# Two attentions with sinks: half of a query projection moved inside the heads, bias rows stored elsewhere, other step tables in two further attentions

## The chip, the cores and the metric

One core of one Trainium2 chip runs the whole program. The metric is the time of one execution on the device, in microseconds (us). TensorE (PE, with its weight loads as PEld), VectorE (DVE), ScalarE (ACT) and GpSimd (POOL) each walk an order of their own; SyncE (SP) issues the weight transfers.

## The reference

Two models one after the other, over 256 tokens of width 1024. The first has four layers: a mixer, a layer norm, a swiglu feed-forward (inner width 2816) and a layer norm. Layers 0 and 3 mix by `mixer_a`, windowed attention with 16 query heads, 4 key/value heads and a learned sink per head; layer 1 is a dilated attention in three groups (`mixer_b`), layer 2 a full causal one (`mixer_c`). Two hybrid layers follow, which the change leaves in their order. Of `mixer_a`:

```python
def mixer_a(x, w_qkv, b_qkv, sinks, w_o, b_o, cos, sin):
    B, S, _ = x.shape
    nq, nkv = A_HEADS * HEAD_DIM, A_KV_HEADS * HEAD_DIM
    qkv = x @ w_qkv + b_qkv
    q = apply_rope(qkv[..., :nq].reshape(B, S, A_HEADS, HEAD_DIM), cos, sin)
    k = apply_rope(qkv[..., nq:nq + nkv].reshape(B, S, A_KV_HEADS, HEAD_DIM), cos, sin)
    v = qkv[..., nq + nkv:].reshape(B, S, A_KV_HEADS, HEAD_DIM)
    o, _ = block_attention(q, k, v, WIN_BLK, A_WINDOW - 1, True, sinks)
    return o.reshape(B, S, nq).astype(x.dtype) @ w_o + b_o
```

The sink is a logit that joins each head's maximum and denominator.

## The kernel before, in words

**Products.** The tokens are two row tiles (t = 0, 1) of 128. A weight chunk is 1024 rows by 512 columns; SP brings it to one of three slots of `raw`. A float32 product is taken as three: the chunk is split into a rounded `whi` (ACT, L1292, half a chunk at a time, or POOL, L1226, in quarters) and the rest `wlo` (DVE, L1715, half a chunk), the rows of x likewise, and each of 8 K-steps is three matmuls of 128x512 (hi·hi, lo·hi, hi·lo). So a projection of one row tile is 24 matmuls, of both 48: L2561 in `product`, or L2577 in `three`, by which a layer's first products and the output projection go.

**One list of stages.** The host code adds stages to a list written by hand; every engine walks the list in order and takes its own part of each stage, tied to the others by semaphores. Nothing is reordered at run time: what stands behind a waiting instruction on its engine waits too.

**Attention with sinks.** Three chunks: one with keys and values, two with queries. After each, DVE adds the bias from PSUM (`biased`, L1821, with the row `abias` in the large buffer `arena`) and rotates the first quarter of every head (`rotated`, L1840 to L1843, in the scratch rows `r`); PE turns the heads (`turn_heads`, L2528, PSUM banks T0 and T1), and ACT copies them into `arena` (L1313). DVE also adds the output bias `abo` to x (L1982). The last query chunk is projected for both row tiles ahead of the heads. Then `spread` does the heads, one unit per head, in 20 steps:

- even step i: PE `scores_of_two(i)` for units i and i+1 (L2793), which takes two of the banks S0, S1, L0, L1 in turn;
- DVE `maxima(i)` (L2093 sets the sink's columns, L2098 adds the mask and takes the maximum), `reciprocal(i-1)` (L2111), `copies(i-3)` (L2106, from a T bank to `pts`);
- ACT exponentials (L1485) and the first scale (L1493), POOL the second scale (L1235);
- PE `turned(i-3)` (L2804), and in odd steps `values_of_two` (L2817) of a pair whose two copies are in.

A bank is free when its reader is done: a T bank when DVE's or ACT's copy is, an S or L bank when both maxima of its unit are. After each four heads ACT rounds the group (L1320) and DVE takes the rest (`group_low`, L1736). `parts` are pieces of the output projection that PE does inside the heads, `rest` those behind them; `lows` and `splits` say in which step DVE splits which chunk.

**Dilated and full.** `paired` does heads in pairs (scores, L2734 turned, L2755 values, DVE's copies L2213); `fill` gives the steps over which a projection is spread inside the heads, as a triple (first step, end of row tile 0, end of row tile 1).

**Between layers.** `renorm` normalises row tile 1 last (DVE L1790, which raises `x_ready`), while PE is already at the next layer's first products of row tile 0; PE then turns x (L2516), and DVE takes xt's low half (L1729) before PE can go on with row tile 1.

## Time and profile before

| | |
|---|---|
| median of 3 runs | 2402.16 us (2400.73 to 2404.18) |
| the profiled execution | 2401.17 us |
| its span | 2399.0 us |
| TensorE's granted clock | 1.00 of full speed |
| PE busy | 2354.6 us, 98% |
| DVE busy | 1636.2 us, 68% |
| ACT busy | 1137.8 us, 47% |
| POOL busy | 225.4 us, 9% |

The span runs from the first to the last instruction that the profiler records. The busy shares are averages over unlike stages; the idle time of PE, by place, is what they leave out.

### The profile page before, as it was taken

Reading aid. Unit: us, or ns where it says so; the run is one execution under the profiler, and the core shown is the slowest. Engines: PE = TensorE matmul, PEld = TensorE weight load, DVE = VectorE, ACT = ScalarE, POOL = GpSimd, SP = SyncE. Lnnn points to the kernel's source line nnn. Section 1 sums busy time; section 2 is a strip of 40 time slices with the busy share of each in tenths; the row PEclk is TensorE's granted clock in tenths of the full one; section 3 lists DMA queues with packets and bytes.
Section 4 is the critical chain, followed back from the end, with each engine's and each line's share of the span. In section 5 each row is a group of like instructions: output and inputs, shape, how many; then the busy total and the mean of one; then the engine's idle time right before and its main releaser. Section 6 shows DMA issues by size and latency. Waiting matters only on the chain.

```text
span 2399.0 us, 31702 instructions
## 1 busy us (share of the span) xinstructions
PE 2354.6 (98%) x12768; PEld 1980.5 (83%) x12768; DVE 1636.2 (68%) x2282; ACT 1137.8 (47%) x1523; POOL 225.4 (9%) x238
## 2 busy tenths in 40 slices
PE   7999999999999999998999999999999999999999
PEld 6788888887888778886888888888888888988887
DVE  7766755557667676677776777777676577687664
ACT  5543345554433544435443455564444365574442
POOL 2400002012000220003100100100100001001000
PEclk9999999999999999999999999999999999999999
DMA  6465343335553455643754344444755344445652
GB/s 250 143 204 207 141 176 141 141 141 176 202 202 141 176 176 193 211 147 122 263 195 174 137 176 159 158 177 148 280 187 182 119 162 158 174 176 186 226 173 91
DMA packets 259072, 418.97 MB, mean 175 GB/s; under 512 B 11984, under 2 KB 149200, under 8 KB 258928
## 3 DMA queue, kind: packets, MB, share of 16 engines
q1 hardware_dynamic: 254064, 400.15, 47.1%
q0 software_dynamic: 4864, 16.80, 2.2%
q8 instruction: 103, 1.69, 0.3%
q14 instruction: 41, 0.34, 0.0%
HBM read 415.86 MB, written 1.05 MB: 174 GB/s over the span
## 4 chain that ended last, share of the span: by engine, by line
PE 89%; DVE 5%; ACT 2%; DMA 1%; issue 1%; POOL 0%; SPq 0%; DVEq 0%; ACTq 0%
PE bank_L L2561 19%; PE bank_L L2577 16%; PE bank_S L2981 8%; PE bank_T L2946 7%; PE bank_L L2946 7%; PE bank_O L2981 7%; PE bank_L L2558 4%; PE bank_T L2951 4%; PE bank_L L2951 4%; PE bank_S L2577 1%; DVE wlo L1715 1%; PE bank_S L2561 1%; PE bank_O L2561 1%; PE bank_T L2528 1%; PE bank_T L2516 1%
## 5 line engine op out<-in xcount | busy, mean ns | idle before, releaser
L1715 DVE TENSOR_TENSOR wlo<-raw,whi 128x2048 fp32r<-128x2048 f32 x316 | 717.5, 2290 | 119.6 <-ACT whi L1292 119.1
L1292 ACT ACTIVATE whi<-raw 128x2048 fp32r<-128x2048 f32 x290 | 542.3, 1894 | 46.8 <-DMA raw<-in_w_in 12.5
L2561 PE MATMUL bank_L<-whi,xt 128*128 128x512 f32 (+2 forms) x1632 | 495.2, 386 | 0.9 <-DVE wlo L1715 0.8
L2577 PE MATMUL bank_L<-whi,xt 128*128 128x512 f32 x1152 | 359.3, 393 | 2.5 <-DVE xt L1729 1.8
L2561 PEld LDWEIGHTS bank_L<-whi,xt 128*128 128x128 f32 x1632 | 296.5, 188 | 57.7 <-issue 2.8
L2561 PE MATMUL bank_L<-wlo,xt 128*128 128x512 f32 (+2 forms) x816 | 311.6, 382 | 0.0
L1587 ACT ACTIVATE tok<-tok 128x256 f32<-128x256 f32 x96 | 40.1, 417 | 449.7 <-DVE tok L2267 449.7
L2577 PEld LDWEIGHTS bank_L<-whi,xt 128*128 128x128 f32 x1152 | 213.3, 188 | 48.0 <-issue 2.7
L2577 PE MATMUL bank_L<-wlo,xt 128*128 128x512 f32 x576 | 225.0, 391 | 0.0
L2946 PE MATMUL bank_T<-xt,whi 128*128 128x512 f32 x768 | 192.4, 393 | 0.0
L2946 PE MATMUL bank_L<-xt,whi 128*128 128x512 f32 x768 | 191.8, 392 | 0.0
L2267 DVE TENSOR_REDUCE tok<-bank_L 128x256 f32<-128x512 f32 x96 | 66.3, 691 | 175.8 <-PE bank_L L2951 175.8
L2561 PEld LDWEIGHTS bank_L<-wlo,xt 128*128 128x128 f32 x816 | 153.5, 188 | 30.1
L2946 PEld LDWEIGHTS bank_L<-xt,whi 128*128 128x128 f32 x768 | 140.8, 189 | 26.9
L2946 PEld LDWEIGHTS bank_T<-xt,whi 128*128 128x128 f32 x768 | 138.3, 189 | 24.6
L2253 DVE TENSOR_TENSOR dlo<-draw,dhi 128x1024 fp32r<-128x1024 f32 x132 | 155.4, 1219 | 3.4 <-ACT dhi L1577 3.4
L1577 ACT ACTIVATE dhi<-draw 128x1024 fp32r<-128x1024 f32 x132 | 131.4, 1045 | 0.0
L2577 PEld LDWEIGHTS bank_L<-wlo,xt 128*128 128x128 f32 x576 | 108.2, 188 | 22.9
L2558 PE MATMUL bank_L<-xt,whi 128*128 128x256 f32 x640 | 118.1, 286 | 0.0
L2267 DVE TENSOR_REDUCE tok<-bank_T 128x256 f32<-128x512 f32 x96 | 66.0, 688 | 74.1 <-PE bank_T L2951 74.1
L1343 ACT ACTIVATE tok<-bank_L 128x512 f32<-128x512 f32 x68 | 40.5, 597 | 152.3 <-PE bank_L L2561 105.9
L2951 PEld LDWEIGHTS bank_L<-xt,wlo 128*128 128x128 f32 x768 | 104.8, 190 | 7.5
(380 smaller groups left out, 3792.2 us busy)
## 6 DMA issues: line engine op xcount, KB each, us to landing
raw<-in_w_gate_up SPq DMA_DIRECT2D x176, 512.0 KB, 5.5
raw<-in_w_in SPq DMA_DIRECT2D x72, 1024.0 KB, 6.8
draw<-in_w_down SPq DMA_DIRECT2D x44, 1024.0 KB, 6.1
raw<-in_ffn_w_up SPq DMA_DIRECT2D x88, 512.0 KB, 5.6
raw<-in_b_w_qkv SPq DMA_DIRECT2D x36, 1024.0 KB, 7.0
draw<-in_ffn_w_down SPq DMA_DIRECT2D x22, 1024.0 KB, 6.0
raw<-in_w_lift SPq DMA_DIRECT2D x16, 1024.0 KB, 6.5
raw<-in_a_w_qkv SPq DMA_DIRECT2D x12, 1024.0 KB, 8.3
```

The lines of the kernel that those rows point to most:

```text
L1292: act.activation(wide(whi, w, nkc, ncols)[:, ks, :], wide(raw, w, nkc, ncols)[:, ks, :], ACT.Copy) \
L1343: act.activation(st["dst"][:, t, :], ps[:, 0:st["ncols"]], st["func"]).then_inc(aev, 1)
L1577: act.activation(dhi[d % 2, k][:, :], draw[:, d % 2, k, :], ACT.Copy).then_inc(dhi_done, 1)
L1715: dve.tensor_tensor(wide(wlo, w, nkc, ncols)[:, ks, :], wide(raw, w, nkc, ncols)[:, ks, :], wide(whi, w, nkc, ncols)[:, ks, :].bitcast(F32 ...
L2253: dve.tensor_tensor(dlo[:, d % 2, k, :], draw[:, d % 2, k, :], dhi[d % 2, k][:, :].bitcast(F32), ALU.subtract).then_inc(dlo_done, 1)
L2267: ins = dve.tensor_reduce(into, banks[UB[q]][:, :].rearrange("p (s c) -> p c s", s=2), AX.X, ALU.add)
L2558: mm = pe.matmul(banks[name][:, o], ww[:, kk, c0:c0 + P], xx[:, kk, :], start=(kk == 0 and q == 0), stop=(kk == nkc - 1 and q == 2))
L2561: mm = pe.matmul(banks[name][:, 0:st["ncols"]], xx[:, kk, t * P:(t + 1) * P], ww[:, kk, :], start=(kk == 0 and q == 0), stop=(kk == nkc - ...
L2577: mm = pe.matmul(banks[bank][:, :], xx[:, k, t * P:(t + 1) * P], ww[:, k, :], start=(k == 0 and q == 0), stop=(k == KC - 1 and q == 2))
L2946: pe.matmul(bank[:, :].rearrange("p (s c) -> p s c", s=2), wh[:, k, cs], xt[:, :, k, :], start=(k == 0), stop=False)
L2951: mm = pe.matmul(bank[:, 0:SEQ], wl[:, k, cs], xt_hi[:, k, :], start=False, stop=(k == KC - 1))
L2981: mm = pe.matmul(banks[ACC[t][h]][:, :], yy[:, 2 * b + k, t * P:(t + 1) * P], ww, start=(j == 0 and k == 0 and q == 0), stop=(j == FJ - 1 ...
```

## The change

1. **Sinks layers (0 and 3).** The last query projection becomes a fill: five K-steps of row tile 0, then the turns of the two earlier tiles, then three K-steps; the 8 K-steps of row tile 1 (24 matmuls) go into steps 0 to 5 of the heads (1, 1, 2, 1, 1 and 2 of them). Row tile 1's bias and rotation are done by DVE in step 6, its turn by PE in step 7, and PE waits for the turned heads ahead of step 8. The scores take two banks, S0 and S1, instead of four. The values of a pair come a step later, in even steps ahead of `turned`, and from unit 16 on behind it. Chunk w1, the first of the output projection, is split by ACT ahead of the heads (`high_ahead`), by DVE half ahead of the first maxima (`low_ahead`) and half in step 3; chunk w1+1 by POOL in quarters after units 2, 3, 5 and 6, by DVE in steps 10 and 18. Pieces of the output projection come at steps 10, 14, 16 and 18 (6, 6, 12, 6 matmuls) instead of 16, 17 and 18 (6, 6, 12).
2. **Homes of the biases.** `abias` goes to the buffer of `pts`, `abo` to that of `sm`, and the last query chunk's row to `bias_q` in `r`, by a third transfer. For layer 3 the first two are issued during layer 2's feed-forward, the third when both row tiles of x are normalised. `biased` waits for all that is issued by then, `bias_q` too, also for keys and values.
3. **Dilated, second half.** The fills end earlier in other steps, the first one's row tile 1 goes to bank O0, a split moves from step 4 to 3, one from 6 to 8, half of one out of step 9, and output pieces begin at step 5 instead of 6.
4. **Full.** The last fill ends at step 5 instead of 6, and output pieces begin at step 5 instead of 6.

```diff
-        abias = arena[:, 3584:3584 + 1536]
-        abo = arena[:, 5120:6144]
...
+        abias, abo, bias_q = pflat, smflat[:, 0:D], r[:, 1, 0:NW]
...
-                                inside=None, into=into, func=ACT.Copy, narrow=None, after=after, skip=0, c0=half * cs,
+                                inside=None, into=into[half], func=ACT.Copy, narrow=None, after=after, skip=0, c0=half * cs,
...
+        def spread(units, ready, first, to, lag, ring, stride, lead=2, fill=(), late=False, needs=None, ropes=None, turns=None,
...
+            values = {}
+            for j in range(len(units) // 2):
+                at = 2 * j + lag + 2
+                values[at + 1 if late and at < len(units) else at] = j
+            last_of = sorted(values)[1::2]
+            st = add("spread", units=units, ready=ready, first=first, to=to, lag=lag, lead=lead, fill=fill, qb=SB if fill else QB,
+                     values=values, late=late, needs=needs or {}, ropes=ropes or {}, turns=turns or {}, pool_highs=pool_highs or {},
+                     lows=lows or {}, highs=highs or {}, parts=parts or {}, rest=rest, out=None, steps=max(values) + 1,
+                     ends={at: g for g, at in enumerate(last_of)})
+            for q in fill:
+                q["kind"] = "fill"
...
-                add("abias", j=j, after=[x_is if i == 0 else (down_done, n["d"])])
-                n["inn"] += 2
+                if i == 0:
+                    biases(j, [x_is])
+                add("bias_q", j=j, after=[x_is if i == 0 else (x_ready, n["xr"])])
+                n["inn"] += 1
...
-                turn(tks[0], k_ok, kT)
+                v_ok = (dev, n["dev"])
                 add("exp_table")
                 add("biased_rows", inn=n["inn"])
                 tk = next_tok()
-                linear(lhs, a_cols(1), NW, "bias", tk=tk, c=1, v=vv, inn=n["inn"])
-                ok = rope(heads(tk), 8, 0, (dev, n["dev"]))
+                late = linear(lhs, a_cols(1), NW, "bias", tk=tk, c=1, v=vv, inn=n["inn"])
+                late["kind"], late["span"], w1 = "fill", (-1, 0, 6), late["w"] + 1
+                ok = (dev, n["dev"])
+                part(late, 0, 5)
+                turn(tks[0], k_ok, kT)
                 turn(tks[1], q_ok, qT[:, 0:4], by=BY)
+                add("high_ahead", w=w1)
+                add("low_ahead", w=w1, half=0)
                 first = (turn_done, n["turn"])
-                behind = [turn(tk, ok, qT[:, 4:8], by=BY)]
+                part(late, 5, 8)
+                rope_in, ok = rope(heads(tk), 8, 0, ok, inside=True)
+                turn_in = turn_inside(tk, ok, qT[:, 4:8], by=BY)
...
-                pool_splits([n["w"] + 1])
-                att = spread(units, [(turn_done, n["turn"]), (dev, n["dev"])], first, behind, to[0], 3, 5, 400,
-                             lows={18: (n["w"] + 1, (0,))}, parts={16: [(0, 0, 0, 2)], 17: [(0, 0, 2, 4)], 18: [(1, 0, 0, 4)]},
-                             rest=[(0, 0, 4, 6), (0, 1, 0, 6), (0, 0, 6, 8), (0, 1, 6, 8), (1, 0, 4, 8), (1, 1, 0, 4), (1, 1, 4, 6),
-                                   None, (1, 1, 6, 8)])
+                hi_by_pool.add(w1 + 1)
+                att = spread(units, [v_ok], first, to[0], 3, 5, 400, fill=[late], late=True, needs={8: (turn_done, n["turn"])},
+                             ropes={6: rope_in}, turns={7: turn_in}, pool_highs={2: (w1 + 1, 0), 5: (w1 + 1, 1)},
+                             lows={3: (w1, (1,)), 10: (w1 + 1, (0,)), 18: (w1 + 1, (1,))},
+                             parts={10: [(0, 0, 0, 2)], 14: [(0, 0, 2, 4)], 16: [(1, 0, 0, 4)], 18: [(0, 0, 4, 6)]},
+                             rest=[(0, 1, 0, 4), (0, 0, 6, 8), (0, 1, 4, 8), (1, 0, 4, 8), (1, 1, 0, 4), (1, 1, 4, 6), None,
+                                   (1, 1, 6, 8)])
...
-                                               ["L0", "L0"])
+                                               [["L0", "O0"], ["L0", "L0"]])
...
-                        att = paired(pairs, first, to=to[1], fill=[(sts[0], (0, 1, 2)), (sts[1], (2, 3, 5))],
-                                     splits={0: (w1, (0,)), 1: (w1, (1,)), 4: (w1 + 1, (0,)), 6: (w1 + 1, (1,)),
-                                             9: (w1 + 2, (0, 1))},
-                                     parts={6: [(0, 0, 0, 2)], 7: [(0, 0, 2, 4)],
-                                            8: [(0, 0, 4, 6), (0, 1, 0, 4), (1, 0, 0, 2)], 9: [(0, 1, 4, 6), (1, 0, 2, 4)]}, **banked)
+                        att = paired(pairs, first, to=to[1], fill=[(sts[0], (0, 0.5, 1)), (sts[1], (1, 3, 5))],
+                                     splits={0: (w1, (0,)), 1: (w1, (1,)), 3: (w1 + 1, (0,)), 8: (w1 + 1, (1,)),
+                                             9: (w1 + 2, (0,))},
+                                     parts={5: [(0, 0, 0, 2)], 6: [(0, 0, 2, 4)], 7: [(0, 0, 4, 6)],
+                                            8: [(0, 1, 0, 4), (1, 0, 0, 2)], 9: [(0, 1, 4, 6), (1, 0, 2, 4)]}, **banked)
...
-                             fill=[(late[0], (0, 0.5, 1)), (late[1], (1, 2, 3)), (late[2], (3, 4, 6))], ropes=ropes_, turns=turns_,
+                             fill=[(late[0], (0, 0.5, 1)), (late[1], (1, 2, 3)), (late[2], (3, 4, 5))], ropes=ropes_, turns=turns_,
...
                                      7: (w1 + 4, (1,)), 8: (w1 + 5, (0,)), 9: (w1 + 5, (1,))},
-                             parts={6: [(0, 0, 0, 2)], 7: [(0, 0, 2, 4)], 8: [(0, 1, 0, 4), (1, 0, 0, 2)],
-                                    9: [(1, 0, 2, 4), (0, 0, 4, 6), (0, 1, 4, 6)]})
+                             parts={5: [(0, 0, 0, 2)], 6: [(0, 0, 2, 4)], 7: [(0, 1, 0, 2)],
+                                    8: [(0, 1, 2, 4), (1, 0, 0, 2), (0, 0, 4, 6)], 9: [(1, 0, 2, 4), (0, 1, 4, 6)]})
...
+            if i + 1 < DEPTH and (i + 1) % 3 == 0:
+                biases((i + 1) // 3, [(pv_done, n["pv"])])
...
+                        for e in range(2):
+                            if i - e in st["pool_highs"]:
+                                high(*st["pool_highs"][i - e], e)
...
+                elif st["kind"] == "bias_q":
+                    for s_, v in st["after"]:
+                        pool.wait_ge(s_, v)
+                    pool.dma_start(bias_q, a_b_qkv[st["j"], NW:2 * NW].partition_broadcast(P)).then_inc(rows_full, 16)
...
+                        if i in st["ends"]:
+                            group_high(to, at["pv"], st["ends"][i])
+                        if i in st["turns"]:
+                            heads_hi(st["turns"][i])
...
-                    dve.tensor_tensor(st["tk"][:, t, :], ps[:, :], abias[:, c0:c0 + NW], ALU.add).then_inc(dev, 1)
+                    row = (abias[:, 0:NW], bias_q)[st["c"]]
+                    dve.tensor_tensor(st["tk"][:, t, :], ps[:, :], row, ALU.add).then_inc(dev, 1)
...
+                        if i - 1 in st["ends"]:
+                            group_low(to, st["ends"][i - 1])
                         if 0 <= i - lag < len(U):
                             copies(i - lag)
+                        for late, t in inside_ends(st["fill"], i - 1, st["steps"]):
+                            if late["evac"] == "bias":
+                                biased(late, t, LB[t])
+                        if i in st["ropes"]:
+                            rotated(st["ropes"][i])
                         if i in st["lows"]:
...
+                        ahead = st["late"] and i <= len(U)
                         if i == st["lead"]:
-                            for late in st["behind"]:
-                                turn_heads(late)
                             for s_, v in st["ready"]:
                                 pe.wait_ge(s_, v)
+                        if i in st["needs"]:
+                            pe.wait_ge(*st["needs"][i])
                         if i < len(U) and i % 2 == 0:
                             scores_of_two(i)
+                        if i in st["values"] and ahead:
+                            values_of_two(2 * st["values"][i])
                         if 0 <= i - lag < len(U):
                             turned(i - lag)
-                        if i > lag and (i - lag) % 2 == 0:
-                            values_of_two(i - lag - 2)
+                        if i in st["turns"]:
+                            turn_heads(st["turns"][i])
+                        if i in st["values"] and not ahead:
+                            values_of_two(2 * st["values"][i])
+                        for late, a, b in inside_step(st["fill"], i, st["steps"]):
+                            if a < b:
+                                product(late, a, b)
                         for piece in st["parts"].get(i, ()):
                             output(st["out"], *piece)
-                        for late, a, b in filled(st["fill"], i, st["steps"]):
-                            product(late, a, b)
```

PE inside the heads of layer 0, before (L2793 scores, L2804 turned probabilities, L2817 values): two pairs of units in steady state.

```order
L2804 MATMUL bank_T<-ident,sm 128x128 x6
L2817 MATMUL bank_O<-pts,arena 64x256 x2
L2817 MATMUL bank_O<-pts,arena 64x128 x2
L2793 MATMUL bank_S<-arena 128x128 x2
L2793 MATMUL bank_S<-arena 128x256 x2
L2804 MATMUL bank_T<-ident,sm 128x128 x6
L2817 MATMUL bank_O<-pts,arena 64x256 x2
L2817 MATMUL bank_O<-pts,arena 64x128 x2
```

The same engine in the changed kernel (L2858 scores, L2869 turned, L2882 values, L2593 turns of heads), steps 6 to 9.

```order
L2858 MATMUL bank_S<-arena 128x128 x2
L2858 MATMUL bank_S<-arena 128x256 x2
L2882 MATMUL bank_O<-pts,arena 64x256 x2
L2882 MATMUL bank_O<-pts,arena 64x128 x2
L2869 MATMUL bank_T<-ident,sm 128x128 x6
L2593 MATMUL bank_T<-ident,tok 128x128 x8
L2858 MATMUL bank_S<-arena 128x128 x2
L2858 MATMUL bank_S<-arena 128x256 x2
L2882 MATMUL bank_O<-pts,arena 64x256 x2
L2882 MATMUL bank_O<-pts,arena 64x128 x2
```

All scores are now in the S banks; the values stand between scores and turned; the turn of row tile 1's four head pairs stands ahead of step 8's scores.

DVE ahead of the heads, before, to the first maximum (L2093):

```order
L1715 TENSOR_TENSOR wlo<-raw,whi 128x2048 x2
L1821 TENSOR_TENSOR tok<-bank_L,arena 128x512 x2
L1840 TENSOR_TENSOR r<-tok,rope_c 128x128
L1840 TENSOR_TENSOR r<-tok,rope_s 128x128
L1840 TENSOR_TENSOR r<-tok,rope_c 128x128
L1840 TENSOR_TENSOR r<-tok,rope_s 128x128
L1842 TENSOR_TENSOR tok<-r 128x16x8
L1843 TENSOR_TENSOR tok<-r 128x16x8
L2093 COPY sm<-sk 128x2
```

DVE in the changed kernel, from the copy of step 6 to the second maximum of step 7 (L2166 copy, L1879 bias, L1898 to L1901 rotation, L2153 and L2158 maxima):

```order
L2166 COPY pts<-bank_T 128x384
L1879 TENSOR_TENSOR tok<-bank_L,r 128x512
L1898 TENSOR_TENSOR r<-tok,rope_c 128x128
L1898 TENSOR_TENSOR r<-tok,rope_s 128x128
L1898 TENSOR_TENSOR r<-tok,rope_c 128x128
L1898 TENSOR_TENSOR r<-tok,rope_s 128x128
L1900 TENSOR_TENSOR tok<-r 128x16x8
L1901 TENSOR_TENSOR tok<-r 128x16x8
L2153 COPY sm<-sk 128x2
L2158 ISA sm,small<-bank_S,masks,sk 128x128
L2158 ISA small 128x1
L2158 ISA sm,small<-bank_S,masks,sk 128x256
```

The bias add and the rotation of row tile 1 stood ahead of all maxima; now they stand between two units' maxima.

POOL, before, from the end of the set-up through layer 0's heads:

```order
L1186 IOTA arena 128x256
L1188 MEMSET arena 128x1 x8
L1239 DMA arena<-in_a_b_qkv 128x1536
L1240 DMA arena<-in_a_b_o 128x1024
L1226 CAST whi<-raw 128x1024 x4
L1235 TENSOR_SCALAR sm<-sm,small 128x256 x16
```

POOL in the changed kernel, the same stretch:

```order
L1288 DMA pts<-in_a_b_qkv 128x1536
L1289 DMA sm<-in_a_b_o 128x1024
L1293 DMA r<-in_a_b_qkv 128x512
L1281 TENSOR_SCALAR sm<-sm,small 128x256 x3
L1238 CAST whi<-raw 128x1024
L1281 TENSOR_SCALAR sm<-sm,small 128x256
L1238 CAST whi<-raw 128x1024
L1281 TENSOR_SCALAR sm<-sm,small 128x256 x2
L1238 CAST whi<-raw 128x1024
L1281 TENSOR_SCALAR sm<-sm,small 128x256
L1238 CAST whi<-raw 128x1024
L1281 TENSOR_SCALAR sm<-sm,small 128x256 x9
```

The four casts of w1+1 stood ahead of the scales; now they stand among them, and a third bias transfer ahead.

## Rows read from the trace of the kernel before

**Rows 1.** Waits of PE over the whole span (us in total, times, longest)
```profile
PE bank_O L2817 <- DVE pts L2106: 9.6, 12, 1.2
PE bank_T L2804 <- ACT sm L1493: 4.5, 6, 1.2
...
PE bank_O L2755 <- DVE pts L2213: 3.2, 3, 1.4
PE bank_O L2755 <- ACT arena L1343: 2.9, 2, 1.8
```

**Rows 2.** Windows over the heads, layers 0 and 3 (busy us by engine)
```profile
48.00:87.00 39.00, 31.25 (x228) 21.33 (x227) 30.29 (x125) 23.82 (x88) 18.06 (x18) 1.00 0.17 55
...
1107.00:1144.00 37.00, 28.71 (x218) 19.48 (x216) 28.62 (x123) 23.65 (x87) 16.37 (x18) 1.00 0.18 58
```

**Rows 3.** PE timeline, layer 0 (start us, us, engine, line)
```profile
39.22 0.71 PE L2561 MATMUL bank_L<-whi,xt 128*128 128x512 f32 x2
...
50.22 1.04 PE L2528 MATMUL bank_T<-ident,tok 128*128 128x128 f32 x8
...
69.60 0.87 PE L2817 MATMUL bank_O<-pts,arena 128*64 128x256 f32 x8 [0.51 <-DVE pts L2106]
70.40 0.93 PE L2793 MATMUL bank_S<-arena 64*128 64x128 f32 x8
71.25 1.00 PE L2804 MATMUL bank_T<-ident,sm 128*128 128x128 f32 x6
...
82.75 0.49 PE L2804 MATMUL bank_T<-ident,sm 128*128 128x128 f32 x3
...
86.73 0.74 PE L2577 MATMUL bank_L<-whi,xt 128*128 128x512 f32 x2
```

**Rows 4.** DVE timeline, layer 0
```profile
27.59 4.48 DVE L1715 TENSOR_TENSOR wlo<-raw,whi 128x2048 fp32r<-128x2048 f32 x2
...
50.49 0.69 DVE L1821 TENSOR_TENSOR tok<-bank_L,arena 128x512 f32<-128x512 f32 x1 [0.50 <-PE bank_L L2561]
...
52.56 0.16 DVE L2093 COPY sm<-sk 128x2 f32<-128x2 f32 x1
52.96 0.35 DVE L2098 CUSTOM_DVE_ANT_0 sm<-bank_S,masks,sk 128x128 f32<-128x128 f32 x1 [0.23 <-PE bank_S L2793]
...
58.13 0.20 DVE L2093 COPY sm<-sk 128x2 f32<-128x2 f32 x1
...
59.00 0.54 DVE L2106 COPY pts<-bank_T 128x384 f32<-128x384 f32 x1
59.46 0.22 DVE L2093 COPY sm<-sk 128x2 f32<-128x2 f32 x1
...
76.84 0.47 DVE L2098 CUSTOM_DVE_ANT_0 sm<-bank_L,masks,sk 128x256 f32<-128x256 f32 x1
...
83.35 0.56 DVE L2106 COPY pts<-bank_T 128x384 f32<-128x384 f32 x1 [2.57 <-PE bank_T L2804]
```

**Rows 5.** ACT, DVE and POOL timelines, layer 0: copies of heads and the splits
```profile
50.86 1.08 ACT L1313 ACTIVATE arena<-bank_T 128x512 f32<-128x512 f32 x2 [5.58 <-PE bank_T L2528]
...
41.57 3.71 ACT L1292 ACTIVATE whi<-raw 128x2048 fp32r<-128x2048 f32 x2
...
43.58 5.82 DVE L1715 TENSOR_TENSOR wlo<-raw,whi 128x2048 fp32r<-128x2048 f32 x2 [0.93 <-ACT whi L1292]
...
43.16 8.12 POOL L1226 CAST whi<-raw 128x1024 fp32r<-128x1024 f32 x4 [28.01 <-DMA raw<-in_a_w_o]
```

**Rows 6.** Start of layer 3: DVE and PE timelines, and its DMA issues
```profile
1078.55 1.28 DVE L1790 SCALAR_TENSOR_TENSOR x<-x,small,arena 128x1024 f32<-128x1024 f32 x1
...
1082.39 0.76 DVE L1825 TENSOR_TENSOR tok<-bank_L,arena 128x256 f32<-128x256 f32 x2 [2.56 <-DMA arena<-in_a_b_o]
...
1084.23 0.70 PE L2577 MATMUL bank_L<-whi,xt 128*128 128x512 f32 x2 [1.52 <-DVE xt L1729]
...
arena<-in_a_b_qkv POOLq DMA_DIRECT2D x1, 768.0 KB, 4.4
```

More of the change, by code:

```diff
@@ L458, in attention, with biases @@
             return (o_done, n["o"])
+        def biases(j, after):
+            add("abias", j=j, after=after)
+            n["inn"] += 2
         def pool_splits(ws, after=None):
@@ L519, in paired @@
             return st
[L521 to L530 removed]
+        def spread(units, ready, first, to, lag, ring, stride, lead=2, fill=(), late=False, needs=None, ropes=None, turns=None,
+                   pool_highs=None, lows=None, highs=None, parts=None, rest=None):
+            values = {}
[9 more added lines that the diff above has]
+                q["kind"] = "fill"
             for i, u in enumerate(units):
@@ L1038, in filled, with inside_step, inside_ends @@
                     if a < (q + 1) * per and b > q * per]
+        def inside_step(fill, i, steps):
+            if fill and "span" in fill[0]:
+                return [(st, *portion(st, i)) for st in fill]
+            return filled(fill, i, steps)
+        def inside_ends(fill, i, steps):
+            if fill and "span" in fill[0]:
+                return [(st, t) for st in fill for t in ended(st, i)]
+            return ends(fill, i, steps)
         def ends(fill, i, steps, left=0):
@@ L2023, in _ @@
                     rotated(st)
+                elif st["kind"] == "low_ahead":
+                    split_lo(st["w"], (st["half"],))
                 elif st["kind"] == "last_low":
```

62 lines of the change are left out of this document (31 added, 31 removed).

## The prediction

> **What bounds the kernel now.** I read the list of waits of PE first. PE is busy 98% of the span, so only its idle time (44 us in all, the span less its busy time) can be won, or grow. Most of what has to do with this change is in one list: 9.6 us in which the values wait for DVE's copies and 4.5 us in which the turned probabilities wait for ACT, all in the two layers with sinks, and 3.2 + 2.9 us in which the values of the dilated and full layers wait for a copy or for their own projection [rows 1]. A measurement of this kernel tells about 0.2% (4.8 us) from no change, so the whole prize is some three times that.
>
> Then the windows over the heads. In layer 0 PE works 31.3 of 39 us and DVE 30.3; in layer 3, 28.7 and 28.6 of 37 [rows 2]. The two engines are equally loaded there, and each idles because they take turns: PE's idle time stands ahead of the values, DVE's ahead of the maxima. That is the picture to keep: whatever the change takes off PE's waits, DVE must not become the longer of the two.
>
> Last the timelines of layer 0. The late projection runs 39.22 to 50.22, 48 matmuls at 0.229 us each; the first maximum is at 52.96, the last ends at 76.84 + 0.47 = 77.31, and the heads' stage is over at 86.73 with 24 matmuls of output projection done in it [rows 3, 4]. One unit costs DVE 59.46 - 58.13 = 1.33 us, of which the copy to `pts` is 0.46 [rows 4]; the sink's columns and two maxima are 0.80 and the reciprocal 0.07.
>
> **Sinks layers: the head start.** 24 matmuls of the projection (5.5 us) go inside. By the new order the first turn of heads stands behind five K-steps, so the projection begins at once, about 37.7 in layer 0. 15 matmuls end at 41.1, two turns (0.85 each, the second waiting for ACT's copies to give the T banks back) at 43.2, nine more matmuls at 45.3. ACT takes about 1.08 for two copies and 1.86 for half a `whi` [rows 5], so it has the heads at 43.9 and w1's first half at 45.8. DVE then splits that half ahead of the first maximum: 2.24 us for one half when alone [rows 4], 45.9 to 48.1. The first maximum comes at 48.1 instead of 52.96: **4.9 us earlier**.
>
> **Sinks layers: inside the loop.** DVE gets two splits that were outside the stretch from the first to the last maximum (steps 3 and 10; 2.24 each alone, 2.91 beside POOL's casts [rows 4, 5]; I take 2.9 and 2.2), and bias and rotation of row tile 1, 50.49 to 52.56 = 2.07 [rows 4]. Together 7.2 us against a head start of 4.9, if DVE's own idle time does not take them up. I do not think it does, since DVE is in the chain that closes the loop. With two banks, scores(i+2) need both maxima of the pair before, and the second of these comes behind a copy that comes behind `turned`, which now stands behind the values as well. Per pair: hand-over 0.1; scores 0.85 (71.25 - 70.40) and values 0.80 (70.40 - 69.60) [rows 3]; from the start of a turn to its copy 0.60 (83.35 - 82.75) [rows 3, 4]; copy 0.46; the sink's columns and maxima 0.80. Sum 3.65 us per pair [rows 3, 4], where the old order gives about 3.1, or 3.8 when `group_low` comes in, 3.45 in the mean.
>
> Step by step: scores of step 2 at 50.4, of step 4 at 53.7, of step 6 at 58.8 (the split of step 3 delays its maxima). DVE ends the rotation of step 6 at 63.4, the maxima of step 7 at 64.2 and copies(4) at 64.7, which frees the T bank that the turn of heads needs. PE turns (0.85), ACT copies (1.08, from 0.6 behind the turn's start), and step 8's scores start at **66.7**, 7.9 us after step 6's. In that stretch PE has nothing else in its order. Then step 10 at 70.4, step 12 at 76.2 (with the split of step 10), step 14 at 79.9, last maximum over at 83.5 instead of 77.3.
>
> Behind the last maximum the old kernel needs 9.4 us to the stage's end [rows 3, 4]. With the values of the tail closer behind I take 8.2: stage end 91.7. It then has 30 output matmuls done instead of 24, worth 6 x 0.229 = 1.4, so the old figure to compare is 88.1. **+3.6 us in layer 0**. Layer 3 has the same order, but the wait ahead of its first turn is not there to be saved: **+4.0**. Bounds for each layer: -0.6 if step 8's scores don't wait for the turned heads beyond the loop's own pace (2.2 less) and the values stay out of the chain (0.55 less in four pairs, 2.2), +7.6 if two casts delay a scale by 2.0 each (below).
>
> POOL's casts: four of them, and eight scales stand behind the first. The old run took 8.12/4 = 2.03 each beside DVE's splits [rows 5]. A scale is needed three steps later only, some 5 us, so I cost them at nothing beyond DVE's 2.9; the cover is this lag, and if it goes a cast costs up to 2.0 us where it stands.
>
> What the row shows of DVE and POOL side by side: the split takes 2.91 us in place of 2.24 [rows 4, 5]. The Trainium skill (SBUF — State Buffer, section "SBUF: two separate sides") says that the pair of ports which DVE and GpSimd share is an exclusive lock, held for a whole instruction, against a DVE operation with two inputs in SBUF while GpSimd reads SBUF. The trace agrees as far as the 0.67 us goes. It speaks against this change, which sets casts beside step 3's split and near the rotation. The rule's own result is a rival below.
>
> **Homes of the biases, layer 3.** The first two transfers leave DVE's wait (2.56 us, ending 82.39) [rows 6]. But the third may start only when row tile 1 is normalised, 1078.55 + 1.28 = 1079.8, and `biased` of the keys waits for it too. A broadcast of 768 KB lands after 4.4 [rows 6]; for 256 KB I estimate 4.0, between 1.5 (a third of it, if the bytes set it) and 4.4 (if they don't), nearer the second since so short a transfer is mostly latency. It lands at 1083.9 where DVE began at 1082.39, so **+1.5** (0 to +1.9), as a longer wait of PE for xt in place of the 1.52 us [rows 6], because DVE's xt stands behind `biased`. In layer 0 the third transfer lies ahead of any use: +0.2, at most +0.7 (256 KB more among loads on which the start waits), at least 0.
>
> **Dilated and full.** The stalls of the values are 3.2 us in three places and 2.9 us in two, the longest 1.4 and 1.8 [rows 1]; by their places 3.7 of the 6.1 us are in the second dilated half, the others in the full layer. Earlier ends of the fills remove the two waits for ACT's evacuation (2.9) and the output pieces cover most of the rest; moving them costs nothing, since the matmuls are the same. **-3.0** (0 to -3.7) and **-1.9** (0 to -2.4). At nothing: the copies at step 8 and 9 that go later, with PE fed by output pieces; if w1+2's second half is late, up to 1 us.
>
> **Sum:** 3.6 + 4.0 + 1.5 + 0.2 - 3.0 - 1.9 = +4.4 against the profiled execution's 2401.17, so 2405.6. The median shown, 2402.16, lies 1.0 above that execution; with it the forecast is **2406.5**, just inside what counts as no change.
>
> **Rivals.** *DVE's insertions cost more (slower).* Mechanism: in steps 3 to 7 POOL has casts ahead of scales, DVE waits for the copy behind them and PE for DVE. Price 2.0 per exposed cast [rows 5], one in each layer: 2406.5 + 4 = 2410.5. It decides when a scale ends later than three steps after its maximum, that is over 5 us. For it: POOL takes 16.37/18 = 0.91 per scale [rows 2] plus up to 2.03 per cast, in a unit of 1.8; against it, only four casts.
>
> *Faster.* The turn of heads is ready in time and values run while PE would wait: both layers at -0.6, 2406.5 - 8.8 = 2397.7, less 1.5 if the third transfer hides: 2396.2. For it: PE idles over 8 us in each of these stages [rows 2] and the change fills exactly these slots with 24 matmuls (5.5 us). Against it: DVE is as busy as PE there. It decides when step 8's scores start before 64.5.
>
> *They cancel.* Head start equals insertions: sinks layers at 0, so 2406.5 - 7.6 = 2398.9, no change.
>
> *The lock.* DVE's split and rotation wait for a whole cast where POOL came first, about 0.5 + 0.35 per layer: 2408.2, by the sentence of the skill named above.
>
> *The change doesn't do what it says:* the third transfer is issued no earlier than the two were, so that PE's wait at layer 3's start is not shortened. That is in my sum already.
>
> **How the numbers follow.** Forecast 0.38 (half of its spread above 2407.0): 0.21 same, 0.17 slower. Casts exposed 0.19, slower. Faster 0.17: 0.15 faster, 0.02 same. Cancel 0.20, same. Lock 0.06, slower. Together faster 0.15, same 0.43, slower 0.42. The range takes the faster case's upper half and the casts' to one us beyond its centre: 2397.0 to 2411.5.
>
> **What the profile would show.** Right: in layer 0 the first maximum near 48, a PE gap of some 3 us ahead of step 8's scores put down to ACT's copy of heads, pair periods near 3.65, last maximum near 83; at layer 3's start a wait for xt near 3 us; stalls of values in the dilated and full layers nearly gone. Wrong: step 8's scores before 64.5, or a stage end in layer 0 (less 1.4) before 86.7, or DVE at layer 3 starting `biased` before 1083 on the old clock.

## The result, and the profile after

The changed kernel takes **2416.84 us** (median of 4 runs, 2416.47 to 2419.7), the kernel before 2401.89 (4 runs, 2400.73 to 2404.18): ratio 1.0064, interval 1.0046 to 1.0081. It is 15 us slower; 2406.5 was forecast, with a range that ended at 2411.5. Every median here is one of fast executions; one execution of 4770.68 us, of the kernel with the values put back, is left out.

The first lines of the page of the changed kernel say already what the sum lacked:

```profile
span 2414.6 us, 31702 instructions
...
PE 2365.0 (98%) x12768; PEld 1984.2 (82%) x12768; DVE 1634.5 (68%) x2282; ACT 1138.8 (47%) x1523; POOL 214.9 (9%) x240
```

PE has the same 12768 matmuls and is busy 2365.0 us where it was 2354.6: **10.4 us more busy time for the same work**. Its idle time, span less busy, is 49.6 us where it was 44.4: **5.2 us more**. Together 15.6, the difference of the spans.

The list of PE's waits over the whole span (us in total, times, longest), which answers to [rows 1]:

```profile
PE bank_S L2858 <- DVE small L2158: 15.2, 10, 2.6
...
PE bank_T L2593 <- DVE tok L1901: 5.1, 2, 2.6
...
PE bank_L L2642 <- DVE xt L1786: 3.4, 2, 3.0
...
PE bank_S L2858 <- ACT arena L1366: 1.7, 2, 1.1
```

The waits of values for copies (9.6 us) are gone; new are 15.2 us of scores waiting for the maxima of the pair before, with 5.1 us in which the turn of row tile 1 waits for its rotation.

What made the same work longer shows in the column PEclk, TensorE's granted clock, by windows of the changed kernel (after the length: busy us of PE, PEld, DVE, ACT and POOL with their counts, then PEclk), which answer to [rows 2]:

```profile
48.00:90.00 42.00, 30.62 (x186) 20.68 (x187) 29.14 (x119) 22.44 (x85) 18.21 (x20) 0.84 0.15 51
...
1060.00:1095.00 35.00, 32.02 (x145) 26.07 (x144) 25.46 (x31) 12.73 (x14) 3.90 (x5) 0.95 0.28 98
1108.00:1160.00 52.00, 40.68 (x247) 28.23 (x247) 34.56 (x128) 28.19 (x91) 18.70 (x20) 0.90 0.21 73
```

TensorE's clock has two levels, 2.4 and 1.2 GHz. In the kernel before it was at the upper one in all these stretches; now it falls to the lower in the heads of both layers and at layer 3's start. PE's timeline in layer 0 shows behind what:

```profile
44.61 0.93 PE L2858 MATMUL bank_S<-arena 64*128 64x128 f32 x8
...
49.72 1.66 PE L2858 MATMUL bank_S<-arena 64*128 64x128 f32 x8 [2.60 <-DVE small L2158]
...
59.73 0.93 PE L2858 MATMUL bank_S<-arena 64*128 64x128 f32 x8 [1.25 <-DVE small L2158]
...
64.83 0.66 PE L2593 MATMUL bank_T<-ident,tok 128*128 128x128 f32 x4 [2.57 <-DVE tok L1901]
66.10 0.69 PE L2593 MATMUL bank_T<-ident,tok 128*128 128x128 f32 x4 [0.62 <-DVE pts L2166]
67.85 1.65 PE L2858 MATMUL bank_S<-arena 64*128 64x128 f32 x8 [1.05 <-ACT arena L1366]
69.43 1.55 PE L2882 MATMUL bank_O<-pts,arena 128*64 128x256 f32 x8
...
73.36 1.65 PE L2858 MATMUL bank_S<-arena 64*128 64x128 f32 x8 [0.91 <-DVE small L2158]
74.94 1.55 PE L2882 MATMUL bank_O<-pts,arena 128*64 128x256 f32 x8
...
80.90 0.93 PE L2858 MATMUL bank_S<-arena 64*128 64x128 f32 x8 [2.03 <-DVE small L2158]
...
84.65 0.93 PE L2858 MATMUL bank_S<-arena 64*128 64x128 f32 x8 [1.22 <-DVE small L2158]
...
96.37 0.72 PE L2642 MATMUL bank_L<-whi,xt 128*128 128x512 f32 x2
```

The eight matmuls of a pair's scores take 0.93 us, or 1.66 behind a wait of 2.60, and 1.65 from the waits of 2.57, 0.62 and 1.05 until about 76; the values then take 1.55 for 0.87. A long gap between the scores of steps 6 and 8 is what I had forecast, but I put it down to ACT's copy of the heads, ahead of the scores: 2.57 us of it stand ahead of the turn and go to DVE's rotation, 1.05 to ACT. That work behind the gaps takes nearly twice as long I had not forecast. Not every gap does it: behind the 1.25 ahead of step 6's scores and the 2.03 ahead of step 12's they still take 0.93, and so behind all the gaps inside the heads of the kernel before, none of which is over 1.23.

At layer 3's start, DVE and PE of the changed kernel, and the landing of the third transfer, which answer to [rows 6]:

```profile
1083.98 1.28 DVE L1847 SCALAR_TENSOR_TENSOR x<-x,small,arena 128x1024 f32<-128x1024 f32 x1
1089.29 0.75 DVE L1883 TENSOR_TENSOR tok<-bank_L,pts 128x256 f32<-128x256 f32 x2 [4.02 <-DMA r<-in_a_b_qkv]
```
```profile
1091.11 1.19 PE L2642 MATMUL bank_L<-whi,xt 128*128 128x512 f32 x2 [2.98 <-DVE xt L1786]
```
```profile
r<-in_a_b_qkv POOLq DMA_DIRECT2D x1, 256.0 KB, 3.7
```

The third transfer is issued when row tile 1 is normalised and lands 3.7 us later; DVE waits 4.02 us for it, PE 2.98 instead of 1.52.

### The profile page after: what moved, and what is told of

It is laid out like the page before. It is cut to its first block, busy times and chain, and to the rows that moved or that the text cites. A ratio compares the mean times of both kernels' runs of the same rounds, so it can differ in the third digit from the quotient of the medians.

```text
span 2414.6 us, 31702 instructions
## 1 busy us (share of the span) xinstructions
PE 2365.0 (98%) x12768; PEld 1984.2 (82%) x12768; DVE 1634.5 (68%) x2282; ACT 1138.8 (47%) x1523; POOL 214.9 (9%) x240
## 3 DMA queue, kind: packets, MB, share of 16 engines
HBM read 416.39 MB, written 1.05 MB: 173 GB/s over the span
## 4 chain that ended last, share of the span: by engine, by line
PE 88%; DVE 6%; ACT 2%; issue 2%; DMA 1%; POOL 1%; SPq 0%; DVEq 0%; ACTq 0%
PE bank_L L2626 18%; PE bank_L L2642 16%; PE bank_S L3052 8%; PE bank_T L3017 7%; PE bank_L L3017 7%; PE bank_O L3052 7%; PE bank_L L2623 4%; PE bank_T L3022 4%; PE bank_L L3022 4%; DVE wlo L1772 2%; PE bank_S L2642 1%; PE bank_O L2626 1%; PE bank_S L2626 1%; PE bank_O L2882 1%; PE bank_T L2581 1%
```

## The experiments

Two theories stood at the start. *Clock:* the gaps as such cost about what I forecast, and the lower clock behind them costs the other 10 us. *Waits:* DVE sets the pace, and slow matmuls lie in time in which PE would wait anyway. Each kernel ran beside the kernel before on one chip, and not all on the same (the kernel before took 2401.5 to 2402.9 there), so two changed kernels are best compared by their ratios. From the intervals I estimate the noise of a difference of two ratios at some 0.002, 5 us.

**Fillers.** Matmuls on finished data where PE waits, into a bank that is free at that time. No engine reads their results.

```diff
+                    IDLE = {2: 10, 6: 4, 'turn': 10, 8: 4, 10: 4, 12: 8, 14: 4}
+                    def idle(i):
+                        name = "O1" if i == "turn" or i < 9 else "L1"
...
+                        for k in range(IDLE[i]):
+                            pe.matmul(banks[name][:, :], ww[:, k % 4, 0:P], ww[:, k % 4, :], start=True, stop=True)
...
+                        if st["late"] and i in IDLE:
+                            idle(i)
```

> The changed kernel with matmuls of 128x512 on finished data into a bank that nobody reads, put where PE waits inside the sinks layers' heads (10 ahead of step 2's scores, 4 ahead of step 6's, 10 ahead of the turn in step 7, 4, 4, 8 and 4 ahead of the scores of steps 8, 10, 12 and 14; 44 per layer, some 10 us of PE that lies in its idle time). Nothing else differs. Theory A (clock): PE's idle gaps inside the heads let its granted clock fall to the lower level, and the work behind them takes twice as long; PE's busy time grew by 10.4 us for the same instructions. With the gaps filled the clock stays at 1.00 in the heads, and the kernel is 6 to 9 us faster than the changed one, about 2409. Theory B (waits): DVE sets the pace, the slow matmuls lie in time in which PE would wait anyway; the fillers bring nothing or cost up to 2 us, 2417 to 2419.

Measured 2410.61 us, ratio to the kernel before 1.0035 (1.0021 to 1.0049): 6.2 us less than the changed kernel, with 88 matmuls more. Its windows over the heads:

```profile
48.00:90.00 42.00, 39.29 (x252) 27.84 (x250) 31.92 (x125) 22.85 (x85) 20.44 (x20) 1.00 0.16 51
...
1108.00:1160.00 52.00, 49.27 (x304) 35.40 (x304) 39.53 (x130) 29.33 (x90) 21.55 (x22) 1.00 0.25 80
```

and three of its starts of scores, with its first output matmul behind the heads:

```profile
45.62 0.93 PE L2858 MATMUL bank_S<-arena 64*128 64x128 f32 x8
...
67.64 0.93 PE L2858 MATMUL bank_S<-arena 64*128 64x128 f32 x8 [0.17 <-ACT arena L1366]
...
71.40 0.93 PE L2858 MATMUL bank_S<-arena 64*128 64x128 f32 x8 [0.29 <-DVE small L2158]
...
92.82 0.72 PE L2642 MATMUL bank_L<-whi,xt 128*128 128x512 f32 x2
```

The clock is 1.00 in both heads, a pair takes 71.40 - 67.64 = 3.76 us where the changed kernel took 73.36 - 67.85 = 5.51. The clock theory holds: more work on PE makes the kernel faster. But it is 6.2 us (7 by the ratios), not the 10 that the theory began with. PE is busy 2377.0 us in this profile; less 88 x 0.229 for the fillers that is 2356.8, so 8.2 us of slow work went (an estimate), and some of it had lain in time in which PE would have waited. The start of layer 3, which has no fillers, still has its lower clock (0.95 in 1060 to 1095).

**Old homes.**

```diff
-        abias, abo, bias_q = pflat, smflat[:, 0:D], r[:, 1, 0:NW]
+        abias = arena[:, 3584:3584 + 1536]
+        abo = arena[:, 5120:6144]
+        bias_q = abias[:, NW:2 * NW]
...
```

> The changed kernel with the biases back in their old homes in the large buffer, and their two transfers issued where they were (no third transfer). Theory A (the third transfer comes late, PE waits 2.98 us for xt at layer 3's start instead of 1.52, and then runs some 3.5 us at the lower clock, which costs half of that): 3.2 us under the changed kernel, 2413.6. Theory B (only the wait counts, the matmuls at the lower clock hide nothing and cost nothing): 1.5 under it, 2415.3.

Measured 2414.48, ratio 1.0047 (1.0031 to 1.0062): 2.4 us under the changed kernel, between the two figures. Its clock in 1060 to 1095 is 1.00 again, its longest wait for xt 1.4 us. The trace shows both effects; the size is not clear of noise, with four runs of each kernel.

**Both.**

> The fillers in the heads and the old homes of the biases together: the clock should be 1.00 all through. If the two causes add up: 6.2 + 2.4 under the changed kernel, 2408.2, and what is left above the kernel with the tables alone (2401.0) is 7.2 us, the idle time and the later end of the heads, 3.6 in each layer. If they overlap, more than 2409.

Measured 2409.14, ratio 1.0025 (1.0016 to 1.0034). The mean clock of the run is 1.0. It is 1.5 us below the fillers alone by the medians and 2.4 by the ratios, where 2.4 was expected if the two causes add up; the intervals overlap, so the runs don't decide between adding up and overlapping. What is left at full clock above the tables alone (below) is 8 us, by the ratios 7.9; the sum had 3.6 + 4.0 = 7.6 for the heads.

**Tables only.** The kernel before with the new steps of the dilated and full layers.

```diff
+                        att = paired(pairs, first, to=to[1], fill=[(sts[0], (0, 0.5, 1)), (sts[1], (1, 3, 5))],
...
+                             fill=[(late[0], (0, 0.5, 1)), (late[1], (1, 2, 3)), (late[2], (3, 4, 5))], ropes=ropes_, turns=turns_,
...
```

> The kernel before with parts 3 and 4 of the change alone (dilated second half and full layer: fills, splits, output pieces). In the changed kernel PE's waits there sum to 1.8 and 1.0 us where they were 4.0 and 2.4. All theories: 3.6 us under the kernel before (2398.3 against 2401.9), the sinks layers as before. If instead the whole change is slower because these tables make something late outside the heads, this kernel is not faster.

Measured 2401.04 (11 runs) against 2402.55, ratio 0.9992 (0.9983 to 1.0001): at most a little faster. Its profiled span is 2396.1 where it was 2399.0, but that execution was the fastest of the eleven. PE's waits there, of this kernel:

```profile
PE bank_T L2734 <- DVE pts L2213: 1.1, 1, 1.1
PE bank_O L2755 <- DVE pts L2213: 1.0, 1, 1.0
```

The waits of [rows 1] for ACT's evacuation are gone, one of the three of values for copies is left, and one ahead of the turned probabilities has come; the profile shows some 3 us, the runs 1.5, and their interval takes in both nothing and 3.

**Early tile.**

```diff
-                late["kind"], late["span"], w1 = "fill", (-1, 0, 6), late["w"] + 1
+                late["kind"], late["span"], w1 = "fill", (-1, 0, 4), late["w"] + 1
...
-                             ropes={6: rope_in}, turns={7: turn_in}, pool_highs={2: (w1 + 1, 0), 5: (w1 + 1, 1)},
-                             lows={3: (w1, (1,)), 10: (w1 + 1, (0,)), 18: (w1 + 1, (1,))},
+                             ropes={4: rope_in}, turns={5: turn_in}, pool_highs={2: (w1 + 1, 0), 5: (w1 + 1, 1)},
+                             lows={7: (w1, (1,)), 10: (w1 + 1, (0,)), 18: (w1 + 1, (1,))},
```

> The changed kernel with row tile 1 of the late projection done in steps 0 to 3 instead of 0 to 5 (2 K-steps each), its bias and rotation on DVE in step 4, its turn in step 5 instead of 7 (three steps ahead of its first use), and the split of w1's second half in step 7 instead of 3. Theory A (turn handshake): PE's waits of 2.6 + 0.6 + 1.0 us around the turn of step 7 and ahead of step 8's scores go, DVE's work is the same; 2 to 3 us less idle time per layer, and the clock doesn't fall behind it: 2 x (2.5 + 2) = 9 under the changed kernel, 2408. Theory B (DVE's load sets the pace wherever it stands): the same work only moves, within 2 us of the changed kernel.

Measured 2416.42, ratio 1.0059 (1.0045 to 1.0072), the same as the changed kernel, as theory B had it. The wait only moved, and the split that made room opened another one further on:

```profile
59.40 1.11 PE L2593 MATMUL bank_T<-ident,tok 128*128 128x128 f32 x4 [3.41 <-DVE tok L1901]
...
72.78 1.65 PE L2858 MATMUL bank_S<-arena 64*128 64x128 f32 x8 [3.17 <-DVE small L2158]
```

In both places PE comes to the turn before DVE has ended the rotation and has nothing else to do; moving it two steps brought nothing. My theory of the handshake falls as far as it named the step.

**Four banks.**

```diff
-                late = linear(lhs, a_cols(1), NW, "bias", tk=tk, c=1, v=vv, inn=n["inn"])
+                late = linear(lhs, a_cols(1), NW, "bias", tk=tk, c=1, v=vv, inn=n["inn"], into=OB)
...
-            st = add("spread", units=units, ready=ready, first=first, to=to, lag=lag, lead=lead, fill=fill, qb=SB if fill else QB,
+            st = add("spread", units=units, ready=ready, first=first, to=to, lag=lag, lead=lead, fill=fill, qb=SB if fill and not late else QB,
```

> The changed kernel with the late projection into banks O0 and O1 (free until the values), so that the scores take the four banks S and L in turn as before; output pieces at steps 16, 17 and 18 (6, 6, 12 and 6 matmuls), since the L banks are in use until then. Theory A (banks): with two banks scores(i+2) wait for both maxima of the pair before, which makes the gaps of 1.2 to 2.6 us ahead of the scores (15.2 us in all), and the clock falls behind them. With four the pair's loop is not closed through the banks: 3 to 5 us less idle time per layer and most of the lower clock gone, some 8 to 14 under the changed kernel, 2403 to 2409. Theory B (DVE's load): two splits, bias and rotation inside the loop are what makes it longer, whatever the banks: within 3 us of the changed kernel.

Measured 2413.38, ratio 1.0045 (1.0032 to 1.0059): 3.5 us under the changed kernel, near theory B. The scores no longer wait for maxima, but what stands behind them does. PE's waits of this kernel:

```profile
PE bank_T L2869 <- DVE small L2158: 5.2, 2, 2.7
PE bank_T L2593 <- DVE tok L1901: 5.2, 2, 2.6
```

By their places in the timeline the first are those behind the split in step 10, the second those of the turn: DVE's insertions, met elsewhere. PE also waits 2.1 us, in two places, for a scale of POOL that came late behind a cast; the changed kernel has no such wait. (The expectations name the other edits of this kernel.)

**Late splits, with two banks and with four.**

```diff
-                             lows={3: (w1, (1,)), 10: (w1 + 1, (0,)), 18: (w1 + 1, (1,))},
+                             lows={15: (w1, (1,)), 18: (w1 + 1, (0,)), 19: (w1 + 1, (1,))},
```

> The changed kernel with DVE's splits of steps 3 and 10 (w1's second half, w1+1's first) put to steps 15 and 18, and that of step 18 to 19, where all maxima are done. Everything else as in the changed kernel. Theory A (each split inside the loop adds its whole length, 2.9 and 2.2 us, since the loop runs through DVE, and makes a gap of PE behind which the clock falls): step 12's scores come 5 us earlier, with the clock 3 to 6 us less per layer, 6 to 12 under the changed kernel: 2405 to 2411. Theory B (the splits only move: PE then waits for them at the output projection): within 2 us of it.

> Both: four banks for the scores and the splits out of the loop. What is left of the change inside the heads is bias, rotation and turn of row tile 1, its 24 matmuls, and POOL's casts. Theory A (banks and splits are two causes that add up): 3.4 us less than the kernel with late splits and two banks. Theory B (with the splits gone DVE is early enough that two banks do): the same as that within 1.5 us. If the 24 matmuls inside the heads are worth anything by themselves, this kernel comes below the 2394.7 of the kernel with tables and later values alone; if the turn inside the loop costs more than they bring, it stays above.

With two banks 2412.34 (1.0042, 1.0025 to 1.0059), with four 2407.57 (1.0024, 1.0015 to 1.0034). Late splits bring 4.5 us with two banks and 5.8 with four; four banks bring 3.5 with the splits inside and 4.8 with them out. Together they bring 9.3 us (9.6 by the ratios), which is clear of noise, and so are the 5.8. The steps of 3.5, 4.5 and 4.8 by themselves are not; the four runs of the late splits with two banks lie from 2408.9 to 2415.94. So both are causes by the traces, and by the runs they add up roughly. Both gains are smaller than theory A had them for each alone. The last question of the expectation has a clear answer: 2407.57 is 12.8 us above the 2394.7 of the kernel with tables and later values alone (14 by the ratios). What this kernel has beyond that one costs that much: the matmuls inside the heads with bias, rotation and turn, the new order ahead of the heads, POOL's casts and the homes. Of the 12.7 us between the two profiles, 5.8 are busy time of PE and 6.9 idle. With four banks and no split inside, the turn's wait remains, and the lower clock behind it:

```profile
62.14 0.66 PE L2593 MATMUL bank_T<-ident,tok 128*128 128x128 f32 x4 [2.61 <-DVE tok L1901]
63.42 1.11 PE L2593 MATMUL bank_T<-ident,tok 128*128 128x128 f32 x4 [0.62 <-DVE pts L2166]
65.22 1.65 PE L2858 MATMUL bank_S<-arena 64*128 64x128 f32 x8 [0.69 <-ACT arena L1366]
```

**Values where they were, and values later alone.** First the changed kernel with only the values put back:

```diff
-                att = spread(units, [v_ok], first, to[0], 3, 5, 400, fill=[late], late=True, needs={8: (turn_done, n["turn"])},
+                att = spread(units, [v_ok], first, to[0], 3, 5, 400, fill=[late], late=False, needs={8: (turn_done, n["turn"])},
```

> The changed kernel with the values where they were (in odd steps, behind the turned probabilities, as soon as both copies are in), two banks for the scores kept. Theory A (the values stand in the chain from the scores to the copy that comes ahead of the second maxima, 0.80 us per pair): PE waits for copies again (some 0.5 to 1.2 per pair), but the scores come earlier; 0 to 3 us under the changed kernel, 2414 to 2417. Theory B (the later values are what fills PE's time): PE waits for the copies on top of the scores' waits, 4 to 8 us above the changed kernel.

Measured 2425.03 (three runs, 2424.59 to 2428.28), ratio 1.0095 (1.0079 to 1.011): **8.2 us slower** than the changed kernel (7.4 by the ratios), the upper end of theory B. Its only trace is of the execution of 4770.68 us, in which TensorE was busy 4743 us for the same matmuls, so where the 8 us went is not shown.

Then the opposite, the kernel before with the tables and the later values:

```diff
...
+                        ahead = st["late"] and i <= len(U)
+                        if i in st["values"] and ahead:
+                            values_of_two(2 * st["values"][i])
                         if 0 <= i - lag < len(U):
                             turned(i - lag)
-                        if i > lag and (i - lag) % 2 == 0:
-                            values_of_two(i - lag - 2)
+                        if i in st["values"] and not ahead:
+                            values_of_two(2 * st["values"][i])
```

> The kernel before with parts 3 and 4 of the change (2401.0 measured) and, of part 1, only this: the values of a pair a step later, in even steps between scores and turned. Projection, banks, splits, biases' homes and output pieces as before. PE waits 9.6 us for copies ahead of the values there, and DVE some 0.35 to 0.5 us per pair for the scores behind them. Theory A (with four banks the later values lengthen no chain): the scores come as soon as PE is free, DVE's waits for them go, 1.5 to 2.6 us per layer: 3 to 5 under 2401.0. Theory B (it is the later values that lengthen the loop, four banks or not): 0 to 6 us above.

Measured **2394.74** against 2402.86, ratio 0.9965 (0.9953 to 0.9978): faster than both kernels, and 6.3 us under the tables alone where theory A had 3 to 5. And without the tables:

> The kernel before with one thing of the change alone: in the layers with sinks the values of a pair a step later, in even steps between scores and turned. Tables of the dilated and full layers as before. With the tables the later values made 2394.7, the tables alone 2401.0. Theory A (the two add up): 6.3 us under the kernel before, 2395 to 2397. Theory B (the gain of the later values hung on the tables or on chance between chips): within 3 us of it.

2397.97 against 2402.18, ratio 0.998 (0.9971 to 0.9989): the later values alone are worth some 4 us (theory A had 6.3, theory B under 3). PE's waits, with tables and later values:

```profile
PE bank_T L2810 <- ACT sm L1499: 3.8, 4, 1.2
PE bank_T L2810 <- DVE small L2104: 2.0, 4, 0.6
...
PE bank_T L2810 <- DVE pts L2112: 1.6, 4, 0.4
...
PE bank_O L2823 <- DVE pts L2112: 1.3, 2, 0.7
```

Of the 9.6 us of values waiting for copies [rows 1] 1.3 are left, and 2.0 + 1.6 us have come ahead of the turned probabilities, in waits of at most 0.6; no scores wait for maxima, as they do in the changed kernel. The waits for ACT's scale, up to 1.2 us long, were there before (4.5, now 3.8).

## Why the prediction was wrong

**The failed step is the sum, which has no term for TensorE's clock.** I costed PE's work at the durations of the kernel before, wherever it stood, and wrote of the gap ahead of step 8's scores only that PE had nothing else in its order. The trace of before shows no gap longer than 1.23 us inside the heads and no lower clock there; the forecast had one of some 3 us. The same trace had the price elsewhere, at the start of the program, and I did not use it (kernel before):

```profile
11.73 3.78 PE L2604 MATMUL bank_L<-whi,xt 128*128 128x512 f32 x8 [5.45 <-ACT whi L1292]
...
17.02 2.07 PE L2604 MATMUL bank_L<-whi,xt 128*128 128x512 f32 x8
```

Behind an idle stretch of 5.45 us eight matmuls take 3.78 us, and 2.07 five us later. (PEclk reads 1.00 in both stretches, so the column alone does not find every slow one; the lengths of like matmuls do.) That should have been a rival with a price: PE's work behind the gap at nearly twice its length, for some us. Measured: 10.4 us of PE's busy time in the profile, 6.2 us of the run's time from the heads by the fillers.

**What held, at full clock.** The filler kernel lets the timing be checked without the clock. It begins its scores 1.0 us later than the changed kernel (45.62 against 44.61), before any filler, so taking 1.0 off: step 8 at 66.6 (forecast 66.7), step 10 at 70.4 (70.4), the stage's end at 91.8 (91.7). A pair takes 3.76 us (3.65; my terms add up to 3.61). In the changed kernel itself step 8 came at 67.85 and step 10, behind slow matmuls, at 73.36; the stage ended at 96.37. So in layer 0 the order, the chain of a pair and the insertions were right, and the durations were not; that the gap ahead of step 8 was ACT's was wrong.

**Terms.** PE's idle time: +5.2 us in all, where the sum said +4.4. In it layer 3's wait for xt is +1.46 (forecast +1.5; landing 3.7, taken as 4.0). But the clock falls behind that wait too, and old homes brought 2.4 us, which is not clear of noise. Dilated and full: -4.9 forecast; the profile has some -3, the runs 1.5 with an interval that holds both. That term was too large.

**Bounds.** Mine for the sinks layers held no lower clock, so their upper end (+7.6) rested on casts. That mechanism did not happen: the casts took 1.03 or 1.04 us each, not 2.03, and PE waited for no scale of POOL.

**The port.** DVE's split in step 3 and POOL's cast ahead of it, changed kernel:

```profile
54.61 2.90 DVE L1772 TENSOR_TENSOR wlo<-raw,whi 128x2048 fp32r<-128x2048 f32 x1
```
```profile
54.32 1.04 POOL L1238 CAST whi<-raw 128x1024 fp32r<-128x1024 f32 x1
```

The cast began first and kept its length of 1.04; the split began 0.75 us before its end and took 0.6 more than its 2.29. In the kernel with four banks the split began first, and it is the cast that grew, to 2.64:

```profile
52.94 2.32 DVE L1772 TENSOR_TENSOR wlo<-raw,whi 128x2048 fp32r<-128x2048 f32 x1
```
```profile
53.52 2.64 POOL L1238 CAST whi<-raw 128x1024 fp32r<-128x1024 f32 x1
```

By the rule that I had weighed from the Trainium skill (SBUF — State Buffer, "SBUF: two separate sides"), the one that starts first has the ports for its whole instruction: both traces agree. In the changed kernel the size, with 0.13 more on the rotation, is near the 0.85 per layer that I gave that rival. It was true and small there.

**The values.** I took them to be a link of 0.80 us in the pair's loop and counted it as a loss that a luckier outcome would take away. The runs say the reverse: putting them back costs 8.2 us, making them later gains 4 to 6. The waits of the kernel before and of the kernel with later values fit this account: in the old place PE stood still for DVE's copy, and the scores behind it stood too; in the new one it has values that are ready. For the changed kernel, where the effect is largest, no trace shows it. I compared two chains by their sums and not by which engine stands still in them.

**Still open.** The 15 us are a balance: the changed kernel also holds the tables and the later values, which alone reach 2394.74. Against that it loses 22 us. Banks and splits account for 9.3 of them; 12.8 remain, the homes among them. What the rest is, the turn of row tile 1 behind its rotation, the order ahead of the heads, the casts, was not taken apart. The lower clock in layer 0 of the kernel with later values (last section) was not followed.

## What to carry to other kernels

A gap of PE has two prices, its own length and the slower work behind it; where a change makes a gap longer than any in its stage, look for the nearest one anywhere in the trace and read the work behind it, and a few useless matmuls in the gap show the second price at once. Work for an idle engine should be something already finished by the others (values a step later), not something that loads the engine it waits for (24 matmuls that brought bias, rotation and splits into DVE's loop). A change in parts should be timed in parts: here one part gained 4 to 6 us under a total of +15.

## What the runs showed of the hardware

In layer 0 of the changed kernel the same eight matmuls took 0.93 and 1.65 us, by what PE had done before: waits of 2.60, or of 2.57 with 0.62 and 1.05 close behind, were followed by the lower clock, those of 1.25 and 2.03 were not. At layer 3's start one wait of 2.98 was enough. But the length of a wait settles neither whether nor when. In layer 3 of the same execution the wait of 2.60 is there again; the scores behind it take 0.93, and the slow matmuls begin only 1.8 us later (three in a row last 0.62 and 0.40 us at full clock, 1.06 and 0.63 here):

```profile
1116.43 0.93 PE L2858 MATMUL bank_S<-arena 64*128 64x128 f32 x8 [2.60 <-DVE small L2158]
...
1118.24 1.06 PE L2626 MATMUL bank_L<-whi,xt 128*128 128x512 f32 x2
1119.09 0.63 PE L2626 MATMUL bank_L<-wlo,xt 128*128 128x512 f32 x1
```

At layer 3's start of the early-tile kernel a wait of 2.65 was followed by no lower clock (1.00 from 1080 to 1095):

```profile
1090.33 0.70 PE L2642 MATMUL bank_L<-whi,xt 128*128 128x512 f32 x2 [2.65 <-DVE xt L1786]
```

And in the kernel with tables and later values the wait of 1.23 us in layer 0, which in the kernel before left the clock alone, is followed by scores at the lower clock:

```profile
57.30 0.52 PE L2810 MATMUL bank_T<-ident,sm 128*128 128x128 f32 x3 [1.23 <-ACT sm L1499]
57.74 1.37 PE L2799 MATMUL bank_S<-arena 64*128 64x128 f32 x8
```

With later values but without the tables, which do not touch this layer, the same wait is followed by scores of 0.93:

```profile
59.40 0.52 PE L2810 MATMUL bank_T<-ident,sm 128*128 128x128 f32 x3 [1.23 <-ACT sm L1499]
59.85 0.93 PE L2799 MATMUL bank_S<-arena 64*128 64x128 f32 x8
```

The matmuls ahead of it are the same in all three. So which gap is followed by the lower clock can differ where the work before it does not, and a gain or loss of a few us that comes by it in one profile need not be a kernel's own. What else decides was not tried.
